# Second mixer's input projection and embedding gates: two 512/256-column matmuls per block instead of three of 256, halves added on VectorE

## What is computed

```
h += mixer(rmsnorm(h))                 # layer 0: RG-LRU ("A1", "A2"), layer 1: Mamba-2 SSD ("B1", "B2")
h += swiglu(rmsnorm(h))                # "F1", "F2"
h += sigmoid(rmsnorm(h) W_g) * (p[i] W_p)          # "PL": gate tile, then projection tile

# B1: the input projection of the SSD mixer
zxbcdt = u @ w_in                      # z | x,B,C | dt
xbc = silu(causal_dwconv(xbc, conv_w, conv_b))     # 4 taps
y = ssd_scan(xs, dt, A, Bm, Cm) + D * xs;  y = y * silu(z);  group rmsnorm
```

## Time and profile before

| | |
|---|---|
| time, median of 3 runs | 2776.83 us (2772.21 to 2777.05) |
| span of the profiled execution, first to last instruction | 2772.1 us (the page gives no other time of this execution) |
| median of the runs less that span | 4.7 us |
| TensorE busy | 2698.1 us, 97% |
| VectorE busy | 2087.2 us, 75% |
| ScalarE, GpSimd busy | 1307.9 us (47%), 440.5 us (16%) |
| HBM | 502.33 MB, mean 181 GB/s |
| PL layer 0 | gate evictions from 1087.9 to 1191.3 us |
| B1, first and second half | L1110 and L1117 from 1201.3 to 1461.9 us and 1566.6 to 1819.8 us |
| PL layer 1 | gate evictions from 2660.7 to 2756.0 us |

### The profile page before, as it was taken

How to read it: one execution, slowest core, us unless ns; L and a number is a source line. 1 busy time by engine, 2 the same in 40 slices (tenths; PEclk the granted TensorE clock), 3 DMA queues, 4 the chain that set the end, 5 groups by cost and what they waited for, 6 DMA issues and landing times.

```text
span 2772.1 us, 50755 instructions
## 1 busy us (share of the span) xinstructions
PE 2698.1 (97%) x17359; PEld 2436.3 (88%) x17359; DVE 2087.2 (75%) x2979; ACT 1307.9 (47%) x1762; POOL 440.5 (16%) x474
## 2 busy tenths in 40 slices
PE   7998999999999999999999999999999999999997
PEld 5887888888888888999998999988888888888897
DVE  8988876765676677888896788978767556767776
ACT  5565344444444444445563455644444444444443
POOL 4444210000000111211111011122000000001122
PEclk9999999999999999999999999999999999999999
DMA  5555565656666565555555655555665666665654
GB/s 189 167 164 159 183 196 182 192 178 190 199 190 195 189 190 166 176 180 172 176 181 161 198 168 168 183 159 181 198 187 187 180 199 193 186 194 176 189 179 149
DMA packets 158369, 502.33 MB, mean 181 GB/s; under 512 B 17792, under 2 KB 20160, under 8 KB 157120
## 3 DMA queue, kind: packets, MB, share of 16 engines
q1 hardware_dynamic: 158192, 501.04, 58.1%
q10 hardware_dynamic: 80, 0.07, 0.0%
HBM read 498.88 MB, written 2.16 MB: 181 GB/s over the span
## 4 chain that ended last, share of the span: by engine, by line
PE 81%; DVE 12%; issue 3%; ACT 1%; POOL 1%; DMA 1%; DVEq 0%; SPq 0%; ACTq 0%; POOLq 0%
PE bank L382 41%; PE bank L384 21%; PE bank L365 6%; PE bank L366 6%; PE bank L367 6%; DVE wlo L797 3%; DVE arena L948 2%; DVE arena L946 1%; ACT whi L572 1%; DVE arena L942 1%; DVE arena L1021 0%; PE bank L540 0%; DVE arena L1110 0%; DVE R L854 0%; DVE rinvh L838 0%
## 5 line engine op out<-in xcount | busy, mean ns | idle before, releaser
L382 PE MATMUL bank<-R,whi 128*128 128x512 f32 x5504 | 1931.2, 396 | 36.3 <-DVE R L854 13.3
L797 DVE TENSOR_TENSOR wlo<-wraw,whi 128x1024 fp32r<-128x1024 f32 (+3 forms) x1056 | 1190.4, 1137 | 521.7 <-ACT whi L572 519.5
L384 PE MATMUL bank<-R,wlo 128*128 128x256 f32 x5504 | 1540.1, 280 | 0.0
L572 ACT ACTIVATE whi<-wraw 128x1024 fp32r<-128x1024 f32 (+3 forms) x1056 | 991.8, 947 | 923.8 <-PE bank L384 772.6
L382 PEld LDWEIGHTS bank<-R,whi 128*128 128x128 f32 x5504 | 1036.7, 188 | 281.9 <-DVE wlo L797 16.4
L384 PEld LDWEIGHTS bank<-R,wlo 128*128 128x128 f32 x5504 | 1043.5, 190 | 0.1
L365 PE MATMUL bank<-R,whi 128*128 128x256 f32 x1856 | 535.1, 288 | 15.4 <-DVE wlo L797 12.9
L366 PE MATMUL bank<-R,whi 128*128 128x256 f32 x1856 | 526.4, 284 | 0.0
L367 PE MATMUL bank<-R,wlo 128*128 128x256 f32 x1856 | 526.3, 284 | 0.0
L365 PEld LDWEIGHTS bank<-R,whi 128*128 128x128 f32 x1856 | 357.1, 192 | 23.6 <-DVE wlo L797 17.4
L366 PEld LDWEIGHTS bank<-R,whi 128*128 128x128 f32 x1856 | 357.2, 192 | 2.1 <-issue 1.9
(11 more groups left out here) (166 smaller groups left out, 1418.6 us busy)
## 6 DMA issues: line engine op xcount, KB each, us to landing
wraw<-in_F SPq DMA_DIRECT2D x352, 512.0 KB, 4.1
wraw<-in_B SPq DMA_DIRECT2D x224, 512.0 KB, 3.7
wraw<-in_A SPq DMA_DIRECT2D x96, 512.0 KB, 3.6
wraw<-in_F SPq DMA_DIRECT2D x128, 384.0 KB, 3.1
wraw<-in_F SPq DMA_DIRECT2D x128, 320.0 KB, 3.2
wraw<-in_PL SPq DMA_DIRECT2D x64, 320.0 KB, 3.2
wraw<-in_PL SPq DMA_DIRECT2D x64, 256.0 KB, 2.8
arena<-cs_rows SPq DMA_DIRECT2D x8, 1024.0 KB, 7.2
```

The source lines that it names most:

```text
L382: nc.tensor.matmul(dst.rearrange("p (s t) -> p s t", s=2), whi[:, q % RING, cols], src[:, :, k, :], start=first, stop=False)
L384: mm = nc.tensor.matmul(dst[:, 0:SEQ], wlo[:, q % RING, cols], src[:, 0, k, :], start=False, stop=last)
L572: nc.scalar.activation(whi[:, slot, 0:w * BLOCK], wraw[:, slot, 0:w * BLOCK], ACT.Copy).then_inc(w_hi, 1)
L797: V.tensor_tensor(wlo[:, slot, 0:w * BLOCK], wraw[:, slot, 0:w * BLOCK], whi[:, slot, 0:w * BLOCK].bitcast(F32), ALU.subtract).then_inc(w_ ...
```

## The change

The wide form is now used in B1 and for the gate blocks of PL as well; only PL's two projection blocks (k of 20 and 21) stay narrow. Each eviction in B1 and each gate eviction in PL gets a `fold` in front, and the multiply by the norm's factor then reads SBUF instead of the bank; the bank is released after that multiply as before. The two numbers in `steps` count the added own-waits of VectorE.

```
-WIDE = ("A1", "A2", "F1", "F2", "B2")
@@ piece
-                    if ph["name"] not in WIDE:
+                    if k >= 20 and ph["name"] == "PL":
                         mm = three(dst[:, 0:SEQ], whi[:, q % RING, cols], wlo[:, q % RING, cols], src[:, 0, k, :],
                                    src[:, 1, k, :], first, last)
                         continue
@@ PL, steps 3 and 7
-                                V.tensor_tensor(swi_g[:, j, :], bank[BANKS4[2 * j]][:, 0:SEQ], rinvh[:], ALU.mult
-                                                ).then_inc(bank_free, 1)
+                                fold(BANKS4[2 * j], swi_g[:, j, :])
+                                V.tensor_tensor(swi_g[:, j, :], swi_g[:, j, :], rinvh[:], ALU.mult).then_inc(bank_free, 1)
@@ B1, odd steps
-                                src = bank[BANKS2[q // 2 % 2]][:, 0:SEQ]
+                                src = BANKS2[q // 2 % 2]
...
-                                V.tensor_tensor(cpad[:, nt % 2, 3:3 + SEQ], src, rinv[:], ALU.mult).then_inc(bank_free, 1)
+                                row = cpad[:, nt % 2, 3:3 + SEQ]
+                                fold(src, row)
+                                V.tensor_tensor(row, row, rinv[:], ALU.mult).then_inc(bank_free, 1)
...
-                                V.tensor_tensor(zt[:, j, :], src, rinvh[:], ALU.mult).then_inc(bank_free, 1)
+                                fold(src, zt[:, j, :])
+                                V.tensor_tensor(zt[:, j, :], zt[:, j, :], rinvh[:], ALU.mult).then_inc(bank_free, 1)
@@
-                steps(dve, ph, body, own, {"A1": 26, "B1": 25, "F1": 6, "PL": 0}.get(name, 4))
+                steps(dve, ph, body, own, {"A1": 26, "B1": 35, "F1": 6, "PL": 2}.get(name, 4))
```

## The result

The change takes 2825.51 us, the median of four runs (2809.29 to 2827.8), against 2776.94 for the kernel before on the same chip. The change is slower, as forecast. The forecast was 2808 us, and the median lies 3.5 us above the range for 8 in 10, which ended at 2822. The profiled execution took 2824.99 us, with a span of 2823.3.

What follows compares the result with a forecast made beforehand. VectorE's order was taken to set B1's loop groups and PL layer 0 once folds are added. B1 +22, PL layer 0 +11, PL layer 1 -2 sum to +31: span 2803, median 2808 us; 8 in 10 between 2786 and 2822.

Steps and rivals of the forecast that it cites:

- What bounds the kernel: B1's loop groups go through VectorE then TensorE in turn; PL layer 0 is level; PL layer 1's period is TensorE's.
- The first rival: Whole kernel: the folds are hidden and TensorE is the bound, -26 us and +0.7 at the end, 2752; chance 0.06.
- PL of layer 0, +11: Two folds an iteration lengthen VectorE's chain from 13.15 to 14.6 us: +11 us.
- Loop groups of B1, +3.5 each, 14 together: B1's four loop groups: six folds +4.3 us on VectorE's part, -0.8 on TensorE's, 3.5 us longer each.
- six folds: In a B1 loop group, folds between the eviction of step 1 and the sixth silu: +4.3 us on VectorE's part.
- Last groups, +3.1 each, +0.6 with B2: Last group of each B1 half: +3.1 us, then +0.6 from the late last z tile; two of them +7.4.
- First groups, +1: First groups of B1's halves: second half -1.7 us, first half +3 less 0.2; together about +1.
- The multiply from SBUF, taken as 0: Multiplies behind the folds, now with two SBUF inputs: no stretch from GpSimd taken, bounds 0 to +7 us.
- PL of layer 1, -2: PL layer 1: period falls from 12.96 to between 12.5 and 12.7 us, -3 over eight, +0.7 at the end.
- The second rival: VectorE takes up part of the folds in B1 and PL: +8 us, 2785; chance 0.16 for 2775 to 2795.
- The third rival: B1 and PL: longer waits drop TensorE's clock, +14 us, and A1's stretch adds +7: 2825 or so; chance 0.16.
- A1's stretch: Multiplies with two SBUF inputs beside GpSimd, at A1's median: 0.06 us on each of 112, +7 us.

Runs made afterwards that it cites:

- the gates alone: The changed kernel with B1 put back to the narrow form without folds, so the change stands in PL only: 2789.2 us, ratio 1.0055.
- the second profile: The changed kernel run and profiled again with nothing edited: 2817.39 us over six runs, ratio 1.013, span 2810.0.
- four banks: The changed kernel with B1's tiles taken from four banks instead of two: 2824.14 us, ratio 1.0148.
- B1 alone: The changed kernel with PL put back, so the wide form and folds stand in B1 only: 2818.22 us, ratio 1.0127.
- four banks on the kernel before: The kernel before the change with B1's tiles taken from four banks instead of two: 2775.82 us, ratio 0.9972.
- the best version: The kernel before with the wide form and folds only in B1's z tiles, and four banks for B1's tiles: 2770.95 us, ratio 0.9973.

## Why the prediction was right, step by step

**What bounds the kernel.** Right. The changing phases were held mostly by VectorE's order and not by TensorE: the wide form without its folds saved 5.5 of 25.8 us. The first rival fell with that. In the third group of B1's second half TensorE's waits for VectorE sum to 5.4 us, where some 5 were to be seen, though a part of them is for banks, which the forecast did not name.

**PL of layer 0, +11.** Measured +11.1 and +10.0, and +10.8 with the gates alone.

**Loop groups of B1, +3.5 each, 14 together.** From step 1 to step 1, as the forecast has it, measured +4.0, +3.0, +2.9 and +4.0, 13.8 together (13.6 in the second profile), and the groups take 69.6 to 70.4 us where 70 was the sign. Cut at step 14, as in the table, it is +2.7, +3.5, +2.1 and +3.4. By parts, as means over the four, VectorE's grew by 3.9 us (forecast 4.3) and TensorE's shrank by 0.5 (forecast 0.8). VectorE was back in step by step 1, just, as the forecast said: it waits there for 0.5 us or less.

But that the sum comes out so well is luck, for its terms do not. The pairs of kernels that differ in one thing give, per loop group from step 1 to step 1:

| term | forecast | measured | pair |
|---|---|---|---|
| six folds | +4.3 | +2.8 | before, and folds without the wide form |
| wide form | -0.8 | -0.4 | these folds, and the same with the wide form |
| multiply from SBUF | 0 | +1.05 | that one, and the change |
| sum | +3.5 | +3.5 | before, and the change |

The fold was priced too high, because the instructions behind it got shorter; the wide form's gain was priced at double; and the multiply was priced at nothing.

**Last groups, +3.1 each, +0.6 with B2.** Measured +3.6 and +4.2 to step 14, and the row of B2 did not get longer.

**First groups, +1.** To step 14, as the forecast sums it, the first half's measured +5.6 against +3, the second half's 0.0 against -1.7. Both are partly an effect of the cut, which stands on VectorE. At the next step 1 the second half's group had gained 1.3 us. In the first half 1.4 of the 5.6 us lie ahead of the first eviction, where the kernel with PL's gates alone lost 2.4 with B1 untouched, and 4.2 between it and the sixth silu (43.2 to 47.4 us), six folds by 0.72 as priced. From the first eviction to the next step 1 it is +2.5, near the 3. TensorE's wait for the eviction of step 5 doubled:

```profile
1252.17 0.77 PE L381 MATMUL bank<-R,whi 128*128 128x512 f32 x1 [4.91 <-DVE arena L1111]
```

It is 4.91 us and was 2.44. That shows how late VectorE is and is no cost beside it: with four banks this wait went, waits of 4.27 us for `wlo` and 2.06 for the silu came, and from the first eviction to the sixth silu it was 47.4 us again.

B1 as a whole: +25.0 and +25.5 against +22 with B2.

**The multiply from SBUF, taken as 0.** This is the term that went most wrong: 6.6 to 7.1 us in B1. The bound of +7 has that size by chance. It was 0.06 us on each of 112 multiplies; measured are 0.36 us on the mean of 48, in 19 of which it falls, nothing on the other 64, and part of it given back. The Trainium skill (SBUF — State Buffer, "Who interferes with whom") said that these multiplies would contend, and this trace agrees: 787 ns with two SBUF inputs, 425 with one. The other half of the rule, as the prediction words it, is too wide: L945, whose only 256-column input is in SBUF, still took up to 1.35 us with the multiply on the bank.

**PL of layer 1, -2.** Measured +1.3, +1.1 and, with the gates alone, +1.1. The way was wrong here. The period was to fall to 12.6 and stayed at 12.96. VectorE's chain, 12.7 by my sum, is stretched: four `lo` take 3.73 us here and 3.29 in layer 0. Of the 57 `lo` of this phase 26 take 1.1 us or more, each of them beside a GpSimd instruction, against 12 of 54 before. No run moved GpSimd's work, so that it is the cause I only infer. Without folds the phase gained 1.7.

**The second rival** (VectorE absorbs part of it) fell: the cheapest loop group cost 2.1 us, not 1, and PL of layer 0 twice its 5. Its seed of truth is in the z tiles, where folds are indeed hidden.

**The third rival** (clock) fell in its first part: the mean granted clock is 0.991 in both spans, with nine stretches at the lower level before and ten in the change. Its second part, A1's stretch, is the +7 above. Its 2825 us are the measured median, but by chance: 14 of them were to come from the clock and came from F1 and F2. What it describes was seen with four banks, where a TensorE wait of 2.0 to 4.3 us stands at each drop in B1.

Added up, the forecast missed 3 us in PL of layer 1 and 3 in B1 and B2, with larger misses in B1 that cancel; these 6 us are the difference of 31 to 37. F1 and F2 add 14, which no term had, and the median of the runs lies 2.2 us above the profiled span where 4.7 were taken. That is the way from 2808 to 2825.5.

## What to carry to other kernels

Before trading TensorE work for VectorE work, find in each phase the instruction at which the two meet, and count what stands ahead of it on VectorE: 97% against 75% over the whole span said nothing, since 25.8 us of TensorE were worth 5.5. An instruction added where the engine idles is free (the z tiles). Added in an unbroken chain it costs its whole length, as in PL of layer 0, 1.42 us for two folds, eight times over. Where another engine holds up what stands behind it, it can cost less, as in B1, 2.8 us for six; and a sum that comes out right does not show that its terms are, so measure each by a kernel that has it alone. A wait that one signal carries comes back under the next signal's name when only the signal's cause is relaxed and the engine's order is not.

## What was not expected of the hardware

F1 and F2, the same code in every kernel here, ran at either of two pitches for a whole layer. The windows, first before, then the change in layer 0, then the change in layer 1:

```profile
400.00:500.00 100.00, 100.00 (x579) 87.49 (x578) 69.49 (x90) 45.43 (x55) 7.92 (x9) 1.00 0.62 190
```

```profile
400.00:500.00 100.00, 100.00 (x568) 86.76 (x567) 68.56 (x90) 44.80 (x53) 7.88 (x9) 1.00 0.59 186
...
2300.00:2400.00 100.00, 100.00 (x579) 87.39 (x579) 64.85 (x84) 44.76 (x54) 4.54 (x5) 1.00 0.65 199
```

And the second profile of the change, layer 0:

```profile
400.00:500.00 100.00, 100.00 (x578) 88.15 (x578) 69.69 (x91) 45.41 (x55) 7.89 (x9) 1.00 0.62 194
```

579 matmuls in 100 us are 0.3454 us a block, 568 are 0.3521. The granted clock is 1.00 and TensorE shows no gap in each. It is +7 us a half, +14 us a layer, and one of the two layers or both had it in three of the twelve profiles: in the change, B1 alone, and four banks on the kernel before (the last two in both layers). The same kernel had it once and not the next time, and kernels without the change have it, so it is not the change alone. Whether the kernel shifts the odds is open: of the runs of the five kernels with folds at every tile of B1, 18 of 29 lie more than 10 us above the fastest of their kernel, of all the other runs 36 of 111. So more of the distance between two medians than the 37 us may go with the change. What causes the pitch stays open too; no run varied anything that would tell. For a verdict it means that two runs of one kernel can differ by 14 or 28 us, two and four times what the best version gains.

In B1, beside the folds, a wide block did not reach 0.3454 either. The window of a stretch in which TensorE shows no gap:

```profile
1608.00:1639.00 31.00, 31.00 (x177) 26.93 (x176) 30.04 (x48) 15.72 (x22) 2.49 (x1) 1.00 0.61 203
```

That is 0.350 us a block, against 0.343 without the folds; the narrow form went from 0.356 to 0.358 when the folds came. Whether VectorE's reads of the banks slow TensorE, or this is hidden waiting that the modelled ends cover, these runs don't tell.
